# A small projection moved ahead of attention, and the weight splits behind it, in a two-block transformer kernel

## What is computed

```python
h = x @ w_in[i]                                   # 1024 -> 2116 columns
q, k, v, qi, ki, wi, u, vs = jnp.split(h, ...)    # 512,128,128,256,64,4 | u 512, vs 512
# rope on q, k, qi, ki; index scores; the 64 best keys of each query; attention over them
a_out = dsa_attention(q, k, v, qi, ki, wi)
b_out = spatial_gating(gelu(u), gelu(vs), ...)    # layer_norm(gelu(vs)), 128x128 mix, times gelu(u)
mix = jnp.concatenate([a_out, b_out], -1) @ w_o[i]
x = layer_norm(ALPHA * x + mix, ln1_g[i], ln1_b[i])
gate, up = jnp.split(x @ w_ffn_in[i], 2, -1)
ffn = (silu(gate) * up) @ w_ffn_out[i]
ple = (p[i] @ w_ple[i]) * sigmoid(x @ w_ple_gate[i])   # p: 256 -> 1024, gate 1024 -> 1024
x = layer_norm(ALPHA * x + ffn + ple, ln2_g[i], ln2_b[i])
```

## Time and profile before

| | |
|---|---|
| median of three runs | 1452.9 us (1451.3 to 1455.47) |
| profiled execution, its own time | 1450.07 us |
| its span in the trace | 1448.3 us |
| mean granted TensorE clock | 0.981 |
| TensorE busy | 1352.1 us (93%) |
| VectorE busy | 943.2 us (65%) |
| ScalarE busy | 656.9 us (45%) |
| GpSimd busy | 113.7 us (8%) |

### The profile page before, as it was taken

One profiled execution on the slowest core, in us unless ns is written; L12 is line 12 of the kernel. 1 busy time (PEld: TensorE's weight loads), 2 busy tenths in 40 slices (PEclk: granted clock), 3 DMA queues, 4 the chain that ended last, 5 costly groups with the idle time before them and its releaser, 6 DMA issues.

```text
span 1448.3 us, 16560 instructions
## 1 busy us (share of the span) xinstructions
PE 1352.1 (93%) x6683; PEld 1111.1 (77%) x6715; DVE 943.2 (65%) x1249; ACT 656.9 (45%) x886; POOL 113.7 (8%) x156
## 2 busy tenths in 40 slices
PE   6999999999989999999789898999998978899998
PEld 6767888887967788887589776888876766688886
DVE  4856777766675777774657856766765775554444
ACT  4544533333553543334366444544435544454542
POOL 1010000000020000000223300000003330000000
PEclk9999999999999999999999999999999988999999
DMA  8505677772713567774153204776753430355550
GB/s 345 209 1 203 231 292 290 293 285 98 269 59 116 207 260 291 291 298 181 41 192 135 102 1 145 269 284 248 281 225 141 151 115 1 116 203 178 188 186 29
DMA packets 40236, 269.87 MB, mean 186 GB/s; under 512 B 4544, under 2 KB 4688, under 8 KB 11872
## 3 DMA queue, kind: packets, MB, share of 16 engines
q1 hardware_dynamic: 37712, 259.31, 48.1%
q0 software_dynamic: 2304, 8.46, 1.6%
q10 hardware_dynamic: 144, 1.05, 0.2%
HBM read 267.75 MB, written 1.05 MB: 186 GB/s over the span
## 4 chain that ended last, share of the span: by engine, by line
PE 78%; DVE 11%; ACT 5%; issue 2%; POOL 2%; DMA 1%; DVEq 0%; ACTq 0%; POOLq 0%
PE ps L1375 23%; PE ps L1377 23%; PE ps L1376 23%; PE ps L1400 4%; DVE WB L1699 2%; ACT E L1497 1%; PE ps L1484 1%; PE ps L1388 1%; POOL st L1299 1%; ACT WB L1497 1%; PE ps L1460 1%; DVE st L1893 1%; PE ps L1360 1%; ACT XTH L1497 1%; DVE st L1961 1%
## 5 line engine op out<-in xcount | busy, mean ns | idle before, releaser
L1699 DVE TENSOR_TENSOR WB<-RAW,WB 128x2048 fp32r<-128x2048 f32 (+5 forms) x210 | 453.3, 2161 | 271.7 <-ACT WB L1497 271.5
L1375 PE MATMUL ps<-WB,XTH 128*128 128x512 f32 (+3 forms) x1176 | 457.3, 389 | 33.3 <-DVE XTL L1704 14.0
L1497 ACT ACTIVATE WB<-RAW 128x2048 fp32r<-128x2048 f32 (+5 forms) x210 | 379.8, 1809 | 237.5 <-PE ps L1377 223.1
L1377 PE MATMUL ps<-WB,XTL 128*128 128x512 f32 (+3 forms) x1176 | 447.9, 381 | 0.0
L1376 PE MATMUL ps<-WB,XTH 128*128 128x512 f32 (+3 forms) x1176 | 447.2, 380 | 0.0
L1375 PEld LDWEIGHTS ps<-WB,XTH 128*128 128x128 f32 x1176 | 222.7, 189 | 75.7 <-DVE XTL L1704 14.0
L1377 PEld LDWEIGHTS ps<-WB,XTL 128*128 128x128 f32 x1176 | 222.5, 189 | 38.7
L1376 PEld LDWEIGHTS ps<-WB,XTH 128*128 128x128 f32 x1176 | 223.0, 190 | 34.8
L1375 PE MATMUL ps<-WB,HTH 128*128 128x512 f32 (+1 forms) x452 | 179.3, 397 | 3.2 <-DVE HTL L1780 3.2
L1376 PE MATMUL ps<-WB,HTH 128*128 128x512 f32 (+1 forms) x452 | 178.5, 395 | 0.0
L1377 PE MATMUL ps<-WB,HTL 128*128 128x512 f32 (+1 forms) x452 | 178.5, 395 | 0.0
(11 more groups left out here) (173 smaller groups left out, 1055.2 us busy)
## 6 DMA issues: line engine op xcount, KB each, us to landing
RAW<-W SPq DMA_DIRECT2D x220, 1024.0 KB, 4.9
RAW<-W SPq DMA_DIRECT2D x7, 960.0 KB, 4.7
RAW<-W SPq DMA_DIRECT2D x6, 910.0 KB, 6.5
RAW<-W SPq DMA_DIRECT2D x9, 576.0 KB, 3.5
VEC<-vecd POOLq DMA_DIRECT2D x10, 512.0 KB, 6.0
RAW<-W SPq DMA_DIRECT2D x8, 512.0 KB, 3.3
RAW<-W SPq DMA_DIRECT2D x6, 546.0 KB, 7.0
GB<-xTd ACTq DMA_DIRECT2D x1, 1024.0 KB, 8.4
```

What stands on the lines that cost most here:

```text
L1375: eng.matmul(ps, xh, hi[:, j, c0:c0 + cw], start=first and j == 0, stop=False)
L1377: op = eng.matmul(ps, xl, hi[:, j, c0:c0 + cw], start=False, stop=last and j == n - 1)
L1497: return eng.activation(dst, src, f, **k)
L1699: eng.tensor_tensor(WB[:, it["raw"], 0:w], RAW[:, it["raw"], 0:w], WB[:, it["high"], 0:w].bitcast(F32), ALU.subtract).then_inc(*up("wl", n))
```

## The change

1. In `plan()` the fifth chunk of `w_in` (vs, the half that the gating normalises) comes before the fourth (u), and the two halves of `w_ple` come before `w_o`.
2. `load_sg` (the GpSimd loads of the gating weights and the embeddings) goes ahead of the third chunk and of `load_vec`; `p_split` and `sgw_mask` go ahead of `rope_in`.
3. `sgu_ln` becomes three parts: sums after the two vs items, squares after the first u item, scaling after the second.
4. The embedding projection becomes a filler: its first half stands behind `sel_mask`, its second half behind the first unit's scores. VectorE copies the results to `PLE`, columns 1092 to 2115 of `H`, where ScalarE copied them to `GB`.
5. A flag `hold` keeps splits out of the list from the mask until the gating; each half of the gating then puts one split (an item of `w_o`) ahead of itself.
6. In the output stage, tile 1's residual is followed by tile 0's transposes and then at once by tile 1's layer norm, and the splits come after. In `linear2` of the gate, tile 1's transposes stand after the second item of tile 0 (`mid_at=1`), not the first.
7. Dummy matmuls: `pads` 8 becomes 4, and `first` is 3 in both layers.

```diff
-        all_rows("w_in", i, 1024, (0, 364), (364, 728), (728, 1092), (1092, 1604), (1604, 2116))
+        all_rows("w_in", i, 1024, (0, 364), (364, 728), (728, 1092), (1604, 2116), (1092, 1604))
+        all_rows("w_ple", i, 256, *halves)
         all_rows("w_o", i, 1024, *halves)
-        all_rows("w_ple", i, 256, *halves)
...
+        PLE = H[:, :, 1092:2116]
...
-                    if cur["ahead"] >= cur["pairs"] or not bufs:
+                    if cur["ahead"] >= cur["pairs"] or not bufs or cur["hold"]:
...
-                    elif it is ia[0]:
+                    elif it is ia[mid_at]:
                         mid()
...
-            run(linear("w_in", "x", xt_w, puts[2]))
+            do("load_sg", i, t_pe)
             do("load_vec", i, 2, VEC[:, 2048:3072], vb + 4096, vec_free[2] + hw[0][0:1])
-            do("load_sg", i, t_pe)
...
+            run(linear("w_in", "x", xt_w, puts[2]))
...
             def gelus():
+                yield from gelu(1)
+                do("sgu_sum", i, gw, sgu[0], list(sq["free"]))
+                yield
+                second = gelu(0)
+                next(second)
+                do("sgu_square", i, sgu[0], sgu[1], sgu[2])
+                sq["free"] = [("ln_ss", (i, 1))]
+                yield
+                run(second)
+                do("sgu_ln", i, sgu[1], sgu[2])
+                yield
...
+            def ples():
                 for c in range(2):
                     def put(t, b, done, c=c):
...
+                        do("ple", (i, c, t), t, c, b, [done])
+                        give(b, ("ple", (i, c, t)))
+                    yield from linear("w_ple", "p", [[("pl", i)], [("pl", i)]], put)
+
+            def gating():
+                cur["hold"] = False
+                for gh in range(2):
+                    advance(1)
+                    b, fr = take()
+                    do("gating", i, gh, b, vsw + fr)
+                    give(b, ("gated", (i, gh)))
+                    yield
+
+            do("p_split", i, list(pt_free))
+            do("sgw_mask", i)
+            fill, ple_fill = gelus(), ples()
...
+            run(fill)
             do("sel_mask", i, src, list(sel_free))
             scr["free"] = [("sel", (i, t)) for t in range(2)]
-            run(fill)
-            do("sgu_ln", i, gw, [col(1) for _ in range(2)], [col(1) for _ in range(2)], [col(1) for _ in range(2)],
-               list(sq["free"]))
...
-            do("p_split", i, list(pt_free))
+            cur["hold"] = True
+            next(ple_fill)
...
-                    if c and t:
-                        xt_n[0][:] = to_XT(X, 8, x_n[0], 0)
                     do("residual", (i, c, t), t, c, b, [done] + x_o[t])
                     rw[t].append(("resid", (i, c, t)))
                     give(b, rw[t][-1])
+                    if c and t:
+                        xt_n[0][:] = to_XT(X, 8, x_n[0], 0)
+                        x_n[1] = ln_tile((i, 1, 1), 1, rw[1])
...
-            fill = chain(gating(), out_start())
-            attention(units, 0.125, fill, pads=(8,), first=8 if i else 3)
+            fill = chain(ple_fill, gating(), out_start())
+            attention(units, 0.125, fill, pads=(4,), first=3)
...
-            x_n[1] = ln_tile((i, 1, 1), 1, rw[1])
...
-            for c in range(2):
-                def put(t, b, done, c=c):
-                    do("ple", (i, c, t), t, c, b, [done, sgo])
-                    give(b, ("ple", (i, c, t)))
-                run(linear("w_ple", "p", [[("pl", i)], [("pl", i)]], put))
-
...
-            run(linear2("w_ple_gate", "x", xt_w, [put_g(0), put_g(1)], mid1, pad=(0, 3)))
+            run(linear2("w_ple_gate", "x", xt_w, [put_g(0), put_g(1)], mid1, pad=(0, 3), mid_at=1))
...
-                act(GB[:, t, c * 512:c * 512 + 512], banks[b][:, :], ACT.Copy).then_inc(*up("ple", key))
...
+                eng.tensor_copy(PLE[:, t, c * 512:c * 512 + 512], banks[b][:, :]).then_inc(*up("ple", key))
```

More of the change, by code:

```diff
@@ L409, in linear, with linear2 @@
             yield
-        def linear2(name, lhs, after, evacs, mid, pad=(0, 0)):
+        def linear2(name, lhs, after, evacs, mid, pad=(0, 0), mid_at=0):
             ia, ib = chunk_items(name), chunk_items(name)
@@ new lines, in program, with gelu, put @@
+            gw = []
+            sgu = [[col(1) for _ in range(2)] for _ in range(3)]
+            def gelu(c):
+                def put(t, b, done):
+                    do("gelu", (i, c, t), t, c, b, [done] + gb_free)
+                    if c:
+                        gw.append(("gelu", (i, c, t)))
+                    give(b, ("gelu", (i, c, t)))
+                return linear("w_in", "x", xt_w, put)
+            def gelus():
+                yield from gelu(1)
[9 more added lines that the diff above has]
+                yield
@@ L701, in gelus @@
+            vsw = [("sgu_ln", (i, t)) for t in range(2)]
+            vec_free[2] = list(vsw)
+            sgo = ("gated", (i, 1))
+            def ples():
                 for c in range(2):
                     def put(t, b, done, c=c):
[L703 to L708, removed]
+                        do("ple", (i, c, t), t, c, b, [done])
+                        give(b, ("ple", (i, c, t)))
+                    yield from linear("w_ple", "p", [[("pl", i)], [("pl", i)]], put)
@@ L763, in program @@
                                       blocks=[c * 128 for c in range(2 * per * (t + 1))]))
[L765 to L773, removed]
             rw = [[], []]
@@ L1574, in sel_score, with sgu_sum @@
                 act(E[:, par, 0:2 * nk], banks[b][:, 0:2 * nk], ACT.Relu).then_inc(*up("sel_relu", (i, t, par)))
-            def sgu_ln(i, gw, mean, ss, nb, after):
-                for e in after:
+            def sgu_sum(i, gw, mean, after):
+                for e in after + gw:
                     on.wait_ge(*at(*e))
                 for t in range(2):
-                    for e in gw[t]:
-                        on.wait_ge(*at(*e))
                     if t:
@@ L1617, in soft @@
                     op.then_inc(*up("exp", (n, q)))
-            def ple(key, t, c, b, after):
-                for e in after:
-                    on.wait_ge(*at(*e))
-                act(GB[:, t, c * 512:c * 512 + 512], banks[b][:, :], ACT.Copy).then_inc(*up("ple", key))
             def gate(key, t, c, b, done, _):
@@ L1684, in scalar_program @@
             parts = dict(split=split, x0=x0, setup=setup, turn=turn, halves=halves, ffn_turn=ffn_turn,
-                         modulate=modulate, hin=hin, lat=lat, gelu=gelu, sel_score=sel_score, sgu_ln=sgu_ln,
-                         p_split=p_split, soft=soft, ple=ple, gate=gate, ffn=ffn, relu2=relu2, norm_sq=norm_sq,
+                         modulate=modulate, hin=hin, lat=lat, gelu=gelu, sel_score=sel_score, sgu_sum=sgu_sum,
+                         sgu_square=sgu_square, sgu_ln=sgu_ln,
+                         p_split=p_split, soft=soft, gate=gate, ffn=ffn, relu2=relu2, norm_sq=norm_sq,
                          lambdas=lambdas, lat_sq=lat_sq, mla_k=mla_k, qk_sq=qk_sq, gain=gain, diff_out=diff_out)
@@ L1979, in norm_apply, with ple @@
                 eng.tensor_scalar(MIX[:, t, :], X[:, t, :], ss, None, ALU.mult).then_inc(*up("hn", g))
+            def ple(key, t, c, b, after):
+                for e in after:
+                    on.wait_ge(*at(*e))
+                eng.tensor_copy(PLE[:, t, c * 512:c * 512 + 512], banks[b][:, :]).then_inc(*up("ple", key))
             def gate(key, t, c, b, _, after):
@@ L1984, in gate @@
                 on.wait_ge(*at("ple", key))
[L1985 removed]
+                eng.tensor_tensor(ms, ms, PLE[:, t, c * 512:c * 512 + 512], ALU.mult).then_inc(*own.up())
                 on.wait_ge(*own.at())
```

18 lines of the change are left out of this document (9 added, 9 removed).

## The result

The changed kernel takes 1464.7 us (median; 1464.26 to 1469.3), the kernel before on the same chip 1452.1 us. The ratio is 1.0089, with a 95% interval from 1.0072 to 1.0107: slower by 0.9%, beyond the 0.3% that can be told from no change. The prediction was 1464 (1449 to 1472). The profiled execution took 1464.26 us, its span is 1462.5 us and its mean granted clock 0.969, against 1448.3 and 0.981 before.

The account below looks back on a forecast made before the run. TensorE, busy 93% of the span, was taken to bound the kernel with its work and waits. 2 x (8.6 - 4.45) + 3.2 = +11.5 us on the profiled 1450.07 gives 1461.6; the median 2.8 above makes 1464, range 1449 to 1472.

Parts of the forecast that it names:

- Before the rounds: `p_split` and `sgw_mask` ahead of the rope on VectorE: rope ends 2.7 us later, index scores and rounds shift 2.4 us.
- Attention: Two full splits ahead of the gating, ScalarE's half then VectorE's, delay later units: +8.6 us a layer for selection and attention.
- the one witness in the earlier trace: The one split inside attention before: 1.92 us on ScalarE, with VectorE idle 3.38 us until it starts its own half.
- Rival (a): At k=1 and 2 in attention both splits are hidden and the kernel is faster: 1444 us, chance 0.13.
- Where TensorE waits: Attention: one new wait of 4.8 us before unit 3's transposes, until unit 3's exponentials end.
- rival (c): Clock falls longer and more often, also behind TensorE's 2.4 us wait before unit 3's scores: 1467 to 1475 us, chance 0.12.
- Output stage: Embedding matmuls gone and tile 1's norm unbroken, but a new 3.1 us wait for `XTL`: -4.45 us a layer.
- The clock: Low clock behind two new waits a layer, 1.5 and 1.2 us, less 2.2 us once in layer 1's attention: +3.2 us.

Follow-up runs that it names:

- e7: e1 with `p_split` and `sgw_mask` moved from ahead of the rope to behind the third of eight rounds: 1447.24 us, ratio 0.9955.
- e9: e8 with one wait more: GpSimd's two scale and shift passes begin only when the layer's selection mask is done; 1436.04 us, ratio 0.9878.
- e1: The changed kernel with ScalarE's half of each attention split put one filler step ahead of VectorE's: 1444.75 us, ratio 0.9931.
- e6: e1 with 12 dummy matmuls ahead of the first gate matmuls: 1438.05 us, ratio 0.9897.
- e4: The changed kernel with 11, 10 and 12 more dummy matmuls before unit 3's scores, its transposes and the first gate matmuls: 1460.14 us, ratio 1.0042.
- e8: e6 with `p_split` and `sgw_mask` moved from ahead of the rope to behind the third round: 1443.43 us, ratio 0.9932.

## Why the prediction was right

The forecast, +11.5 us from a circle of two engines in attention, held in place and mechanism; in size it held in part because a clock term that was too small was offset by others. Point by point:

- **Before the rounds.** The rope was to end 2.7 us later and ended 1.7 later (its split at 48.64). `p_split` takes 0.68 us here, not the 1.60 of the earlier trace rows. The term was mis-sized because I took its duration from a place where GpSimd's passes ran beside it; e7 and e9 show that effect on other instructions. So the mask came 0.9 us early, where 0 was predicted.
- **Attention.** At unit 3's maxima the working has +8.9 us, measured from the mask are +8.2; at tile 0's first `w_o` matmuls it has +8.6, and they start at 101.42 and not 93.12, +8.3. Both splits stood exposed with the idle time that the one witness in the earlier trace rows had (3.38 us there, 3.86 and 3.37 here). e1 shows the cause: with the same work and the halves apart the stretch from the mask is 7.4 us shorter. Rival (a), the splits hidden, is thereby what the kernel does when the list allows it.
- **Where TensorE waits.** I had one wait of 4.8 us before unit 3's transposes, released by `E`. There are three, 2.38, 2.25 and 0.88, and the first two are for the gating on VectorE. Their sum is 5.5 us. The wait of 2.4 us that I had kept for rival (c) was real.
- **Output stage.** The wait for `XTL` was predicted at 3.1 us and is 2.95. With the clock the stage gives -2.3 and -3.1 us, predicted -3.25. Without the clock's share (next point) it is -4.7 us in both layers, predicted -4.45: the matmuls saved and the unbroken norm are as worked out.
- **The clock.** Predicted +3.2 us net: 1.5 in each attention and 1.2 in each output stage, less 2.2. This is the term that was mis-sized most. Against e1 it is 1.4 us in attention of layer 0 and 3.7 in layer 1. In the output stages it is 2.4 and 1.6: the 24 gate matmuls take 7.9 us from 135.62 to 143.5, 7.2 in layer 1, and 5.6 at the full clock of e6. Together that is 9.1 us and not 5.4. Over the two layers this error, the early mask (0.9 us twice) and the shorter stretch to unit 3's maxima (0.7 and 0.8 us) offset each other.
- **The second block.** Nothing was predicted there and 3 us came. The marks stand 11.5 us apart at its attention (1205.27 before, 1216.75 after), 13.1 apart at 1232.04 and 1245.16, and 14.2 at the last stretch. Windows over like stretches, before and after, show the clock at 0.76 and 0.61:

```profile
1205.30:1217.30 12.00, 11.95 (x73) 9.25 (x76) 4.27 (x12) 6.02 (x24) 0.00 (x0) 0.76 0.00 0
```

```profile
1216.80:1228.80 12.00, 12.00 (x60) 8.70 (x61) 4.27 (x12) 4.36 (x19) 0.00 (x0) 0.61 0.01 1
```

The same program, with the same wait ahead of it (3.39 and 3.38 us), ran at the lower level for longer. Nothing in this block's program differs, and one kernel's executions differ by as much: 22 of the kernel before, taken beside e1, lie between 1450.7 and 1458.1 us, the longer ones with the lower mean clock (0.975 to 0.976, against 0.979 to 0.982). So the closeness of 1464 to 1464.7 is in part luck: by its own terms the sum stood at +11.2 us, and the kernel before has a median 2.8 us above its profiled execution, which I added and which the one after has not (1464.7 and 1464.26). What sets how long the low stretches last is left open; I have no run that tells.

The Trainium skill (TensorE: Matmul & The Clock Gate, HAM oscillation) prices the low clock at half of the time spent at it. The 17 us at 0.50 in layer 1 make 8.5 us by that, and the stretch was 3.7 us longer than in e1. In layer 0's output stage, where every matmul is on the path, the rule and e6 agree better: 5.4 us at 0.50 make 2.7, and 2.9 were got back.

## What to carry to other kernels

An operation made of two engines' halves, put as one step into in-order programs, makes each engine wait for the other once, and if the second engine owes the first something behind it, they take turns. Put the first half one step earlier. In the trace look for idle time of the second engine before every such instruction, released by the first half; here it was 3.4 to 3.9 us, 1.9 of it the first half itself and the rest what stands ahead of it on its engine. When work is moved out of a stage where it covered a wait, the wait appears in its place and the low clock behind it; dummies get the clock back, at no cost where they end before the wait does (e6), and for what they delay where they don't (e4). When a step is moved in time, look also at what the engines beside it do at the new place: here VectorE and GpSimd held each other up.

## What the runs showed of the hardware

**VectorE and GpSimd hold each other up on SBUF.** `p_split` takes 1.60 us beside GpSimd's passes and 0.68 alone; the split of 1024 columns 2.29 and 1.22; the mask 2.57 and 0.42; GpSimd's pair 3.50 and 2.52. e9 took away the overlap alone, and all three of e7's and e8's durations returned. VectorE's maxima and copies out of PSUM ran beside the same GpSimd passes at their usual 0.75 and 0.69 us, in the changed kernel from 72.46 to 75.49. A small VectorE instruction on SBUF is held up as well: the scaling of the maxima, 128x4 elements, takes 0.73 us beside these passes in e9 and 0.17 without them.

The Trainium skill (SBUF — State Buffer, Who interferes with whom) has a port pair that the two share as an exclusive lock, held for a whole instruction, and a VectorE instruction with two SBUF inputs contends for it. The split reads two operands of SBUF and fits that: begun behind GpSimd's first pass of 1.25 us, it ends about when that pass and its own 1.22 us are over. The mask and the scaling read only one operand of SBUF and were held up too; why is open. No run here shows the lock itself.

**The low clock costs by place.** 5 us of it behind a wait cost 2.9 us where all matmuls are on the path; 17 us in layer 1's attention, where VectorE's and ScalarE's chain also leads, cost 3.7. The time of an unchanged block differs by 3 us between the profiled executions of the kernels before and after, and e6's profiled execution lost 5.4 us on e1's in code that is the same. So a difference of a few us between two kernels is to be looked for in the clock first, and over several executions.
